# Forty U blocks beside the choice of experts, U loads ahead of gate loads, V begun inside U, and three buffers for the weights of V

## What is computed

```python
q = (xb @ w_q).reshape(Tb, 8, 2, 128)
s = jnp.einsum('thpc,hpnc->thpn', q, sub_keys)      # scores against 2 x 128 keys
sv, si = lax.top_k(s, 16)                           # then the best 16 of the 256 pairs
eidx, gate = ..., jax.nn.softmax(top, axis=-1)      # 16 experts for each of 8 heads
act = jax.nn.gelu(einsum('td,thkd->thk', xb, expert_u[eidx]), approximate=False)
out = einsum('thk,thkd->td', gate * act, expert_v[eidx])   # 16384 experts of 1024 numbers
```

## Time and profile before

| | |
|---|---|
| three runs | 2584.79, 2586.67 (median) and 2590.8 us |
| the profiled execution | 2608.19 us, of which the span of its instructions is 2606.4 us |
| PE busy | 2419.6 us, 93% of the span |
| DVE, ACT, POOL busy | 1517.9 (58%), 1287.3 (49%), 1443.5 us (55%) |
| mean granted TensorE clock | 0.966 of full speed |
| DMA | 552.84 MB, mean 212 GB/s |

### The profile page before, as it was taken

One profiled execution on the slowest core, in us unless ns is written; L12 is line 12 of the kernel. 1 busy time (PEld: TensorE's weight loads), 2 busy tenths in 40 slices (PEclk: granted clock), 3 DMA queues, 4 the chain that ended last, 5 costly groups with the idle time before them and its releaser, 6 DMA issues.

```text
span 2606.4 us, 46380 instructions
## 1 busy us (share of the span) xinstructions
PE 2419.6 (93%) x15014; PEld 2198.2 (84%) x15014; DVE 1517.9 (58%) x3071; ACT 1287.3 (49%) x2823; POOL 1443.5 (55%) x1772
## 2 busy tenths in 40 slices
PE   7987998998979999999998898998979999999997
PEld 7876888997979999777886888997979999778885
DVE  2234542898833412587886642898833411578886
ACT  4343534454845555454553534454845555445553
POOL 6633145687658887564310045687658888565320
PEclk9998999999989999999999999999989999899998
DMA  5313422243888876888996431243788876788993
GB/s 192 130 73 122 182 102 86 97 164 105 279 265 266 276 225 202 294 285 311 351 343 237 148 111 74 98 155 117 260 274 268 270 239 193 277 275 310 352 349 131
DMA packets 222551, 552.84 MB, mean 212 GB/s; under 512 B 49697, under 2 KB 137761, under 8 KB 197102
## 3 DMA queue, kind: packets, MB, share of 16 engines
q1 hardware_dynamic: 135854, 404.19, 45.7%
q0 software_dynamic: 31680, 118.06, 12.3%
q10 hardware_dynamic: 54912, 29.37, 3.9%
HBM read 480.91 MB, written 70.65 MB: 212 GB/s over the span
## 4 chain that ended last, share of the span: by engine, by line
PE 72%; POOL 10%; issue 9%; DVE 4%; ACT 2%; DMA 1%; POOLq 0%; another core or an unknown queue 0%; ACTq 0%; DVEq 0%
PE psum L970 26%; PE psum L762 11%; PE psum L763 10%; PE psum L764 10%; POOL w_split L648 10%; PE psum L792 9%; PE psum L1018 2%; PE psum L954 1%; DVE arena L1398 1%; DVE arena L1610 1%; DMA gain_rows<-gains 0%; DVE uT_split L1405 0%; DMA w_ring<-peer_v 0%; PE psum L1054 0%; POOLq L647 0%
## 5 line engine op out<-in xcount | busy, mean ns | idle before, releaser
L648 POOL TENSOR_TENSOR w_split<-w_ring,w_split 128x256 fp32r<-128x256 f32 x1152 | 886.7, 785 | 274.9 <-ACT w_split L1231 217.8
L762 PE MATMUL psum<-uT_split,w_split 128*128 128x320 f32 x2560 | 817.9, 320 | 43.3 <-POOL w_split L648 31.7
L763 PE MATMUL psum<-uT_split,w_split 128*128 128x320 f32 x2560 | 798.0, 312 | 0.0
L764 PE MATMUL psum<-uT_split,w_split 128*128 128x320 f32 x2560 | 798.0, 312 | 0.0
L1231 ACT ACTIVATE w_split<-w_ring 128x256 fp32r<-128x256 f32 x1152 | 474.5, 418 | 504.9 <-PE psum L764 457.7
L762 PEld LDWEIGHTS psum<-uT_split,w_split 128*128 128x128 f32 x2560 | 487.5, 190 | 61.6 <-POOL w_split L648 43.0
L970 PE MATMUL psum<-v_hl,p_hl 128*128 128x512 f32 x2064 | 493.0, 394 | 24.9 <-DVE p_hl L1842 15.9
L763 PEld LDWEIGHTS psum<-uT_split,w_split 128*128 128x128 f32 x2560 | 488.0, 191 | 0.0
L970 PEld LDWEIGHTS psum<-v_hl,p_hl 128*128 128x128 f32 x2064 | 391.5, 190 | 113.6 <-DVE p_hl L1842 19.4
L764 PEld LDWEIGHTS psum<-uT_split,w_split 128*128 128x128 f32 x2560 | 487.0, 190 | 0.0
L1824 DVE TENSOR_TENSOR arena<-arena 128x256 f32<-128x256 f32 x256 | 166.8, 682 | 439.6 <-ACT arena L1332 397.1
(11 more groups left out here) (265 smaller groups left out, 2284.7 us busy)
## 6 DMA issues: line engine op xcount, KB each, us to landing
w_ring<-peer_u SPq DMA_DIRECT2D x128, 1024.0 KB, 5.2
w_ring<-peer_v SPq DMA_DIRECT2D x256, 512.0 KB
arena<-gates SPq DMA_DIRECT2D x32, 1024.0 KB, 8.2
gates<-w_ring POOLq DMA_DIRECT2D x22, 1024.0 KB, 6.7
weighed<-arena ACTq DMA_DIRECT2D x40, 512.0 KB
arena<-weighed SPq DMA_DIRECT2D x40, 512.0 KB
w_ring<-w_pq SPq DMA_DIRECT2D x8, 2048.0 KB, 8.1
gates<-arena POOLq DMA_DIRECT2D x10, 1024.0 KB, 8.5
```

The source lines that it names most:

```text
L648: pool.tensor_tensor(wq[:, q, 1], quarter(raw, m, q), wq[:, q, 0].bitcast(F32), ALU.subtract).then_inc(w_lo_ready, 1)
L762: pe.matmul(bank[:, 0:TOK], hi, uT_hi[:, k, :], start=k == 0, stop=False)
L763: pe.matmul(bank[:, 0:TOK], hi, uT_lo[:, k, :], start=False, stop=False)
L764: last = pe.matmul(bank[:, 0:TOK], lo, uT_hi[:, k, :], start=False, stop=k == KD - 1)
```

## The change

- `AHEAD` goes from 32 to 40, so `EARLY` is 56, `LATE` 72, and `ROUNDS` 9. ACT makes the exponentials after U block 28 instead of 32 (`EXP_AT`), PE turns the gates after block 31 (`TURN_AT`), and nine more blocks follow before gb.
- SP issues the third U load behind one gate load, and the fourth behind two gate and two V loads, where both came behind three gate and four V loads.
- In the last round of ur, ACT makes `vhi(0)`, `p_high(0)`, `vhi(1)`, and DVE `v_low(0)`, `p_low(0)`, `v_low(1)`. The last comes before the last `weigh`.
- `phl` gets a third buffer, in space of `uT_split`.
- The first two P loads go from block 9 of V, both together, to blocks 32 and 42.
- Rows have eight slots, not nine. POOL first waits for the stored activations, then fetches 16 activations with a row behind every second one; before, four rows came ahead of that wait, five behind it, and then the 16 activations. Picks are added in blocks 12 to 115.
- The fold runs ahead of V block 120, and its addition to x at block 125.

```diff
-AHEAD = 32
+AHEAD = 40
+TURN_AT = 31
+EXP_AT = 28
-SLOTS = 9
+SLOTS = 8
-FIRST_STEP = 14
+FIRST_STEP, LAST_STEP = 12, 116
-        phl = view(p_hl, 0, 2, 2 * NP_)
+        phl = [view(p_hl, 0, 2 * NP_), view(p_hl, 2 * NP_, 2 * NP_), view(uT_split, 2 * D, 2 * NP_)]
...
+                def v_load(b):
+                    if b >= 4:
+                        sp.wait_ge(v_split, NB * l + b - 3)
+                    sp.dma_start(v_raw[b % 4], V[b // 2][:, b % 2]).then_inc(v_loaded[b % 4], 16)
+
                 g_load(0, CATCH)
+                u_load(first + 2)
                 g_load(2, 0)
+                v_load(0)
+                v_load(1)
+                u_load(first + 3)
                 g_load(1, CATCH + 1)
-                for b in range(4):
-                    sp.dma_start(v_raw[b], V[b // 2][:, b % 2]).then_inc(v_loaded[b], 16)
+                v_load(2)
+                v_load(3)
...
-                    if c == 4:
+                    if b in (EARLY - 24, EARLY - 14):
...
+                        p_load((b - EARLY + 24) // 10)
...
                 pool.wait_ge(w_lo_ready, split_base(l, HP + NB))
-                for k in range(SLOTS):
-                    if k == 4:
-                        pool.wait_ge(acts_stored, 16 * (NB // 4) * (l + 1))
-                        pool.wait_ge(weighed_stored, 16 * (LATE // 4) * (l + 1))
-                        pool.wait_ge(early_made, EARLY * (l + 1))
-                    gather_row(k)
                 pool.wait_ge(acts_stored, 16 * (NB // 4) * (l + 1))
                 for k in range(16):
                     gather_act(k)
+                    if k == 7:
+                        pool.wait_ge(weighed_stored, 16 * (LATE // 4) * (l + 1))
+                        pool.wait_ge(early_made, EARLY * (l + 1))
+                    if k % 2:
+                        gather_row(k // 2)
...
-                with pe.Fori(0, AHEAD // 4) as i:
+                with pe.Fori(0, EXP_AT // 4) as i:
...
+                for b in range(EXP_AT, TURN_AT):
+                    split_block(None, 0, split_base(l, HP + b), a_bank(AJ[f"up{l}"] + b))
                 for t, (off, rows) in enumerate(TILES[:2]):
                     pe.wait_ge(picked_ready, 2 * l + t + 1)
...
+                for b in range(TURN_AT, AHEAD):
+                    split_block(None, 0, split_base(l, HP + b), a_bank(AJ[f"up{l}"] + b))
...
                 for n in range(2):
                     pe.wait_ge(acc_copied, 2 * l + n + 1)
                     pe.matmul(psum[0:NS, n, :], fold, acc_tmp[:, n, :], start=True, stop=True).then_inc(d_filled, 1)
+                for b in range(120, NB):
+                    v_block(l, b // 6, b % 6)
...
-                    act.wait_ge(v_summed, (NB + 2) * l + b + 1)
-                    act.activation(phl[:, b % 2, 0:NP_], p_block(b), ACT.Copy).then_inc(p_hi_ready, 1)
+                    act.wait_ge(v_summed, (NB + 2) * l + max(b, 2))
+                    act.activation(phl[b % 3][:, 0:NP_], p_block(b), ACT.Copy).then_inc(p_hi_ready, 1)
...
+                        if last and r == 4:
+                            vhi(0)
+                            p_high(0)
+                        if last and r == 6:
+                            vhi(1)
...
                         dve.wait_ge(a_emptied, AJ[f"ur{l}"] + 8 * j + r + 1)
+                        if j == ROUNDS - 1 and r == 5:
+                            v_low(0)
+                            p_low(0)
+                        if j == ROUNDS - 1 and r == 7:
+                            v_low(1)
                         weigh(s_act[:, r // 4, r % 4, 0:NP_], j % 2, r).then_inc(late_made, 1)
```

More of the change, by code:

```diff
@@ L31 @@
 CATCH = EARLY // 8
+PAIR_USES = [len(range(s, ROUNDS, 2)) for s in range(2)]
 GC = 16
@@ L73 @@
 G_JOBS, U_JOB = (0, 1, 2, 4), 3
[L76 removed]
+FIRST_STEP, LAST_STEP = 12, 116
 def steps_at(b):
[L81 removed]
+    at = [min(PICKS, max(0, -(-PICKS * (n - FIRST_STEP) // (LAST_STEP - FIRST_STEP)))) for n in range(b, b + 2)]
     return range(*at)
@@ L1024, in peer @@
                 for n in range(4):
-                    last = pe.matmul(psum[:, 2 + n, :], phl[:, 0, 0:P], vhl[0][:, 0, 0:512], start=True, stop=False,
+                    last = pe.matmul(psum[:, 2 + n, :], phl[0][:, 0:P], vhl[0][:, 0, 0:512], start=True, stop=False,
                                      skip_group_check=True)
@@ L1031, in peer @@
                         split_block(i, 4, split_base(l, HP + EARLY + r), a_bank(AJ[f"ur{l}"] + r, i, 4))
-                with pe.Fori(0, NB // 6) as i:
+                with pe.Fori(0, 20) as i:
                     for r in range(6):
                         v_block(l, i, r)
-                for b in range(NB // 6 * 6, NB):
-                    v_block(l, NB // 6, b % 6)
                 pe.wait_ge(a_emptied, AJ[f"ur{l}"] + LATE)
@@ L1292, in peer @@
                     act.activation(picked[:, t, 2, :], picked[:, t, 2, :], ACT.Exp).then_inc(exp_ready, 1)
+                for i in range(EXP_AT // 4, AHEAD // 4):
+                    ahead(i)
                 for c in range(GB):
@@ L1320, in store_group, with p_high, vhi @@
                                   ).then_inc(weighed_stored, 16)
+                def p_high(b):
+                    if b < EARLY:
+                        act.wait_ge(early_made, EARLY * l + b + 1)
+                    elif b % 8 == 0:
+                        k = (b - EARLY) // 8
+                        act.wait_ge(p_loaded[k % 2], 32 * (PAIR_USES[k % 2] * l + k // 2 + 1))
+                    act.wait_ge(v_summed, (NB + 2) * l + max(b, 2))
+                    act.activation(phl[b % 3][:, 0:NP_], p_block(b), ACT.Copy).then_inc(p_hi_ready, 1)
+                def vhi(b):
+                    act.wait_ge(v_loaded[b % 4], 16 * (NB // 4 * l + b // 4 + 1))
+                    act.wait_ge(v_summed, (NB + 2) * l + max(b, 2))
+                    act.activation(vhl[b % 3][:, 0, :], v_raw[b % 4], ACT.Copy).then_inc(vhi_ready, 1)
                 def late_round(i, last=False):
@@ L1856, in peer @@
                         gather_step(l, k)
-                dve.wait_ge(rows_used, PICKS * (l + 1))
-                for n in range(2):
-                    dve.tensor_copy(acc_tmp[:, n, :], psum[:, 6 + n, :]).then_inc(acc_copied, 1)
+                    if b == LAST_STEP:
+                        dve.wait_ge(rows_used, PICKS * (l + 1))
+                        for n in range(2):
+                            dve.tensor_copy(acc_tmp[:, n, :], psum[:, 6 + n, :]).then_inc(acc_copied, 1)
+                    if b == 125:
+                        for n in range(2):
+                            dst = x[0:NS, 2, n * 512:(n + 1) * 512]
+                            full(DJ[f"fold{l}"] + n)
+                            dve.tensor_tensor(dst, psum[0:NS, n, :], dst, ALU.add).then_inc(d_emptied, 1)
                 dve.wait_ge(v_summed, (NB + 2) * (l + 1))
@@ L1868, in peer @@
                                                  op0=ALU.mult, op1=ALU.add).then_inc(acc_emptied, 1)
-                for n in range(2):
-                    dst = x[0:NS, 2, n * 512:(n + 1) * 512]
-                    full(DJ[f"fold{l}"] + n)
-                    dve.tensor_tensor(dst, psum[0:NS, n, :], dst, ALU.add).then_inc(d_emptied, 1)
             memory(0)
```

80 lines of the change are left out of this document (31 added, 49 removed).

## The result

The changed kernel takes **2553.0 us** (median of four runs, 2551.5 to 2553.9). The kernel before takes 2586.0 in the same comparison. The ratio is 0.9868 with an interval of 0.9851 to 0.9885: 33 us are gained, where 68.5 were forecast. It is faster, as expected, but by half as much, and outside the range.

What follows compares the result with a forecast made beforehand. PE, busy 2419.6 of 2606.4 us, bounds the kernel; only idle time and lower clock can be won. 7.5 + 13.7 + 25.3 + 22.6 = 69.1 gives 2539.1 profiled, less 21.5: 2517.6, say 2518 us; range 2498 to 2540.

Steps and rivals of the forecast that it cites:

- short waits for P: In V: PE waits briefly for split P with two buffers; the third buffer takes most of this, 1.0 us left.
- V's term: V from the last U matmul: 359.6 us a layer, saving 8.8 and 13.8, together 22.6 us.
- the constant difference: Last step: runs without a profile lie 21.5 us lower, so 2539.1 us profiled becomes 2517.6.
- The stalls of the P loads: In V: 6 us of stalls when V loads queue behind four P loads; spreading the loads removes them.
- Block 13: In V: PE waits 4.3 us (0 to 10) for the sixteenth activation, then loses 1.9 us to lower clock.
- The rival in which the activations are there in time: V's block 13: no wait for the sixteenth activation, both layers save 4.3 + 1.9 us, 2505 us; chance 0.20.
- Turn and gb: Gate turn and gate products: 7.5 us saved at the turn for two layers, and 13.7 us with gb at its floor.
- the drain that the prediction quotes: At ACT's table loads: the skill adds 1.38 us to every switch, 5.5 us more for four; the trace showed no such gap.
- ur: Late U blocks: earlier U loads cut the stall to 3.5 us a layer (1.3 to 5.8), saving 25.3 us.
- The assumption that the clock would not fall there: In ur: the remaining stall, taken as 3.5 us, is too short for the clock to fall.
- The rival "the third P buffer does nothing": In V: short waits come from DVE, the 6 us stay and a like sum joins them, 2540 us; chance 0.12.

Runs made afterwards that it cites:

- the repeat: The kernel before, unchanged, profiled a second time: 2585.2 us, ratio 0.9994; its profiled execution took 2587.4 us.
- V begun late: The changed kernel with all 16 activations fetched before any row, and V's first splits put back behind ur: 2545.8 us, ratio 0.9835.
- P loads alone: The kernel before, with only the first two P loads moved to V blocks 25 and 33, one at a time: 2577.3 us, ratio 0.9965.
- third buffer alone: The kernel before, with only the third buffer for the split P: 2584.4 us, ratio 0.9989.
- fold behind V: The changed kernel with 16 activations before rows, V loads in U's fourth late round, P block 1 split inside U, fold after V: 2522.8 us, best of all.
- activations first: The changed kernel, but POOL fetches all 16 activations first and the eight rows behind them: 2532.6 us, ratio 0.9794.
- first pick at 16: The changed kernel, with picks added to the sum from V block 16 on instead of 12: 2534.3 us, ratio 0.9793.
- the run with one block behind the turn: The kernel before, with exponentials after U block 28, gates turned after block 31 and only block 32 behind the turn: 2569.7 us, ratio 0.9931.

## Why the prediction missed

**The step that failed** is the last one: "The runs without a profile had a median 21.5 us lower; I take the same difference off". It went wrong together with one sentence on V, "The rest are short waits for P, which has two buffers". The 21.5 us were no overhead of profiling. They were V's 19.3 us of extra length in that one execution. The change can't save them in runs that don't have them, and the prediction counted them twice. V's term put them down as a gain, and the constant difference then took the same microseconds off once more. The changed kernel's own difference is −1.5 us.

**A reading that went wrong with it.** The prediction puts the 1.25 us before the block at 1069.59 down to the 2.31 us that ACT waited for a V load. But that wait ended at 1071.38, 1.8 us later. The block at 1069.59 hangs on a `p_high` at 1068.66, behind the first "remote" wait. The stalls of the P loads exist all the same: the repeat has 2.12 and 3.46 us there, and spreading the loads takes them away.

**What was left of V's term.** From the last U matmul, V takes 360.5 and 362.0 us in the repeat of the kernel before (its windows and the 5.02 us ahead of them), and 362.4 and 361.3 in the changed one. Forecast was a gain of 22.6 us; against the repeat it is a loss of 1.3. The runs give the parts, for both layers together:

| part of V | gain, us | from |
|---|---|---|
| begun inside U, with its clock, less the wait at block 1 | +10.8 to +12.5 | V begun late |
| P loads spread | +9 | P loads alone |
| third P buffer | +3 | third buffer alone; within its interval, so not shown |
| fold in the path | −3.9 | fold behind V |
| wait and clock at block 13 | −16.1 to −19 | rows; activations first, first pick at 16 |

The sum lies between −0.1 and +4.5 us; parts measured alone need not add up to the microsecond. So V's edits won some 20 us, and the fold and block 13 gave them back.

**Block 13** was foreseen with its mechanism: 4.3 + 1.9 us a layer, where 5.82 + 2.2 and 5.45 + 2.6 were found. With E, the end of the last U matmul, at 1017.57, the last store was issued at 1019.68, E + 2.1 (forecast 2.2). It landed 4.4 us later, as assumed, and POOL started at E + 7.5 (6.6). Its 22 operations took 30.45 us (30.8). The sixteenth activation, started at 1055.49, released DVE at 1058.84, 3.35 us later; the working had 1.0 + 1.0. From the end of its row on POOL that is 2.4 us. The Trainium skill ("DMA: Bandwidth & Descriptors", Anatomy of one DMA) has about 2.0 us of fixed cost, nearer to it than my 1.0; the row decides. The rival in which the activations are there in time is out as a forecast. But its price for the wait, 2 × 6.2 us, was too low: the wait and the clock behind it are 16.1 us by the rows, and taking it away gave 15.4 and 15.6 us in V and 19 to 20 between medians.

**Turn and gb.** Forecast 21.2, found 17.5 (8.1 and 9.4) against the repeat. The floor of 89.2 us for gb left out 1.0 us that PE waits behind gb in either kernel, ahead of its zeroing matmuls. The wait of 1.17 us before gb's first matmul was not foreseen either. It stands in the run with one block behind the turn as well. The exponentials cost PE nothing, where I had 2.0 us. From the start of the choice stage's U matmuls to the end of block 31 are 116.9 us in the changed kernel, and 120.5 less one block of 3.52 in the repeat. The table load began 0.02 us after the last Gelu once more (timeline of ACT in the changed kernel), and the drain that the prediction quotes does not show:

```profile
616.97 0.21 ACT L1277 ACTIVATE arena<-psum 128x64 f32 x1
617.20 1.28 ACT L1300 ACT_TABLE_LOAD   x1
```

The reason given was wrong, though the sum was near: "the nine blocks behind the turn cover DVE's copies and one-hots". One block is enough; the other eight are worth 2 us.

**ur.** Forecast 25.3, found 18.9 against the repeat, 20.9 from profile to profile. What is left was put at 3.5 us a layer. The waits came in four pieces, 5.0 and 3.9 us together, and by its windows ur stands 6.1 and 5.0 us above its floor of 253.4. The mechanism was right, and the term too large: the waits that are left were taken at 7.0 us over both layers and are 8.9, and another 2 us stand in no wait of over 0.25 us. The assumption that the clock would not fall there held: behind the longest of them, 2.21 us, the granted clock is 1.00.

**The sum again:** 17.5 + 18.9 − 1.3 = 35.1, beside 33.0 measured. From profile to profile the three terms (turn and gb, ur, V) were 4.0, 4.4 and 4.5 us too large, together the 12 to 13 us. The other 23 are the one execution. The side (faster) was right, and so were the places where the changed kernel waits. The rival "the third P buffer does nothing" came nearest, at 2540, but for a reason that did not hold: it had the short waits stay, when in ordinary executions they do not occur.

## What to carry to other kernels

When the profiled execution lies outside the timed runs (here 21.5 us above the median, with runs from 2584.8 to 2590.8), the excess is somewhere in its rows, and must be found before any wait there is counted as a gain. Look for waits whose releaser is nothing of the kernel, or price the change once with them and once without, and let the range hold both. When a stage starts earlier, everything asked for at a fixed block of it is asked for earlier too: here moving the first pick by four blocks is worth 15 us of V by the rows, and 19 by the medians, more than either of V's two edits that do gain. And before a cover is made large, try the smallest one: one block did what nine were brought for.

## What the hardware showed

- A TensorE wait of a few microseconds can cost 2 to 3 more in clock, but its length alone does not say whether it does. After 5.02 us, 24 matmuls take 8.1 to 8.5 us for 5.45; after 5.82 us, 12 take 4.91 for 2.73; after 2.12 us, 12 take 4.59. After the waits of 1.64 us, 12 take 3.02, where a row of 12 at full clock shows 2.88. But with the third P buffer alone a wait of 2.78 us was followed by 3.06, nearly full speed, and the 2.21 us in ur by matmuls of 0.41 and 0.31 us at a clock of 1.00. What decides it was not found. The row of that 2.78 us wait, then a window of PE behind block 13's wait in the changed kernel, most of it at the lower level of 1.2 GHz, and one behind ur's 2.21 us:

```profile
1070.43 3.06 PE L970 MATMUL psum<-v_hl,p_hl 128*128 128x512 f32 x12 [2.78 <-DVE p_hl L1842]
```

```profile
1060.71:1066.00 5.29, 5.29 (x15) 0.61 0.57 191
782.44:786.00 3.56, 3.56 (x24) 1.00 1.09 391
```

- One of fourteen profiled executions had eleven ACT waits tagged "remote", nine of them 2 to 5 us long, and was 20 us longer in V. What they are was not found.
- Work that no variant touches, from the start to the end of the matmuls ahead of layer 0's attention, ended between 444.5 us (the best variant) and 452.4 (V begun late). So profiled spans of two variants are compared stage by stage, not as a whole.
